# Half-row gathers on 128 partitions, a fourth k-step of expert 28 loaded ahead, and half of the last norm's row spread ahead of a product

## The chip, the core and the metric

One core of a Trainium2 chip runs the whole program. The metric is the device time of one execution in microseconds (us), as the median of several runs. Engines are named as in the profile: PE is TensorE, DVE VectorE, ACT ScalarE, POOL GpSimd, SP the queue engine that issues most DMAs; all DMAs of the core run on 16 DMA engines.

## The reference, cut to what matters

The program computes two blocks over 512 rows of 1024 numbers, all in fp32. The first block and the mixer of the second are not touched. Behind them stands a mixture of experts: 32 experts in 4 groups, 2 for each row, each with two matrices of 1024x512 (gate, up) and one of 512x1024 (down), then a last norm.

```python
h = rms_norm_2(x, norm_ffn_g) * (1.0 + sc_f) + sh_f
g = argmax(h @ w_router_group + b_group)                  # one of 4 groups
top_p, top_i = top_k(softmax(expert logits of group g), 2)
for each expert e, for the rows that chose it:
    hid = silu(rows @ w_gate[e]) * (rows @ w_up[e])       # 1024 -> 512
    y  += weight * (hid @ w_down[e])                      # 512 -> 1024
x = x + g_f * y
out = rms(x) * final_norm_g
```

Each expert's weights are 6 MB, 192 MB in all, and every one of them is read once from HBM.

## The kernel before, in words

**Tiles.** The rows of an expert are handled in a tile of at most 64 rows (MT = 64). Where more rows chose an expert, "extra" tiles follow on the same weights (`overflow`, `extras`). The router is a chain of small DVE steps and a few products on PE. At its end stands `slots` (lines 2678 to 2683): for each tile and each of its 64 places the number of the row that belongs there, made by a product of two one-hot tensors on PE (lines 2313 and 2314, 8 products that the profile shows as 16 instructions) and three DVE steps. Places that hold no row get a number past the end, which the gather leaves out. Rows fill a tile from place 0 upwards.

**Gather.** `dve_xn_tile` (line 785) scales the rows of the norm, and POOL stores them to a scratch in HBM (`xn_dram`, line 1960). For each tile POOL copies the tile's column of `slots` to `idx_col` and issues an indirect DMA (`gather`, lines 2891 to 2896): 64 indices, each a row of 4 KB, into 64 partitions of `tile.xg`.

**Turn.** `turn_rows` (line 2972) transposes the 64 gathered rows on PE, 8 transposes of 64x128 with a column stride of 8, into one PSUM bank; `rows_in` (line 3172) on DVE multiplies by the column of the norm's gain and adds the shift, and gives `tile.xT`.

**Products.** `gate_up` (line 2982) runs 8 k-steps of two products; `turn_hidden`, `down` (line 3006) follow. ACT makes the exponentials, DVE the rest (`clamped`, `hidden`, `rows_gated`), and POOL scatters the result with an indirect DMA of 128 half rows of 2 KB (`scatter`, line 2898). The PE stream for expert e is: turn the hidden tile of e-1, gate_up of e, turn the rows of e+1, down of e-1.

**Weights.** Three slots of 6 MB in SBUF (U = 3). SP issues loads in order (`sp_experts`, lines 2794 to 2880): the first three experts (in the order 1, 2, 0) as soon as the earlier phase frees the room, and then for each next expert the first half of gate and up (2 MB) when PE has done the first half of the product that used the slot before, the second half when the whole of it is done, and the down weights when that slot's down product is done. Each issue waits on a semaphore of PE, and the issues behind it on SP's queue wait with it. For expert 28 (AHEAD, the 29th) three of the eight k-steps (512 KB each) are loaded into a tensor of their own, `ahead`, much earlier (line 619), and only the fourth k-step of the first half is loaded in its turn (`load_behind_ahead`, line 2811). The last expert's second half comes as two quarters.

```python
def load_behind_ahead(u):
    eng.dma_start(wgu[u][:, 0, AHEAD_STEPS:4, :, :], A["w_gu"][AHEAD, :, 0, AHEAD_STEPS:4, :, :]
                  ).then_inc(w_gu[u][0], 16)
```

**Room.** `xg` of the three tiles are `yflat[0:64, 0:3072]`, that is yT, free once the mixer's output product is done; POOL clears them first (line 2887). `gain_row` and `ones_row`, for the last norm, lie on partition 64 of the same room.

**The end.** For the last expert (e = 31) PE runs turn_hidden and down of expert 30 ahead of gate_up of 31, and between them `spread_gain` (line 3085): two products that spread the 1024 gains of the last norm from one row to 128 partitions, which ACT copies to SBUF. When expert 30 is scattered, SP reads all results back (line 2872), DVE adds them (`add_rows`), PE sums with expert 31's rows straight from SBUF, and ACT and DVE make the last norm.

Of the kernel before, what the change touches and what calls it, by code (L numbers as in the profile page):

```python
# [75 lines left out]
def build_program(nc, A):  # L76
# [7 lines left out]
    with ctx:  # L84
# [696 lines left out]
        def dve_xn_tile(i, t):  # L781
            V.wait_ge(s_sq_rows, NORM0 + TT * (i - 1) + t + 1)
            if i == 2 and t >= 2:
                V.wait_ge(s_xnst, 16 * (t - 1))
            dve.done(V.tensor_scalar(xn_tiles[i - 1][t], X[:, t, :], rstd[:, t:t + 1], None, MUL))
            V.sem_inc(s_xn, 1)
# [1352 lines left out]
        def pe_block2(eng):  # L2139
# [173 lines left out]
            for n in range(2 * TT):  # L2313
                last = T.matmul(bank[0:MT, 0:NE + NOV], hot_pos[:, n, :], hot_tile[:, n, :], start=n == 0, stop=n == 2 * TT - 1)
# [273 lines left out]
        slots = sb("slots", [MT, NE + NOV + 2], u32)  # L2588
# [5 lines left out]
        xn_dram = nc.dram_tensor("xn_scratch", [SEQ, DM], fp32, kind="Internal").ap()  # L2594

# [6 lines left out]
        def dve_router(eng):  # L2602
# [76 lines left out]
            v = r_v[0:MT]  # L2679
            done(V.tensor_scalar(v, bank[0:MT, 0:NE + NOV], 0.0, 1024.0, ALU.is_equal, MUL))  # L2680
            empty(V, "dve", V.scalar_tensor_tensor(v, bank[0:MT, 0:NE + NOV], -1.0, v, ADD, ADD), ("slots",))
            done(V.tensor_copy(slots[:, 0:NE + NOV], v))
# [26 lines left out]

        def gate_up_weights(u, e, k):  # L2710

            if isinstance(e, int) and e == AHEAD and k < AHEAD_STEPS:
                return ahead[:, k, :, :]
            return wgu[u][:, k // 4, k % 4, :, :]
# [20 lines left out]
        tiles = [Tile(u, yflat[0:MT, 1024 * u:1024 * u + 1024], hflat[:, 512 * u:512 * u + 512],  # L2735
                      hflat[:, 1536 + 256 * u:1792 + 256 * u], yflat[:, 3072 + 256 * u:3328 + 256 * u],
                      hflat[:, 2304 + 512 * u:2816 + 512 * u]) for u in range(U)]
        extra = Tile("extra", side[0:MT, 0:1024], side[:, 1024:1536], side[:, 1536:1792], side[:, 1792:2048],
# [15 lines left out]
        idx_col = sb("idx_col", [MT, U + 1], u32)  # L2754
# [39 lines left out]
        def sp_experts(eng):  # L2794
# [16 lines left out]
            def load_behind_ahead(u):  # L2811
                eng.dma_start(wgu[u][:, 0, AHEAD_STEPS:4, :, :], A["w_gu"][AHEAD, :, 0, AHEAD_STEPS:4, :, :]
                              ).then_inc(w_gu[u][0], 16)

# [3 lines left out]
            def next_gate_up(u, e):  # L2818
# [6 lines left out]
                if isinstance(e, int) and e == AHEAD:  # L2825
                    load_behind_ahead(u)
                else:
# [27 lines left out]
            for u, e in enumerate(FIRST):  # L2855
# [3 lines left out]
                load_down(u, e)  # L2859
            eng.wait_ge(s_routed, 1)  # L2860
# [22 lines left out]
        def pool_experts(eng):  # L2883
            done = pool.done
            done(G.memset(ones_row, 1.0))
            eng.dma_start(gain_row, A["final_g"].rearrange("(o n) -> o n", o=1)).then_inc(s_gateB, 16)
            done(G.memset(yflat[0:MT, 0:3072], 0.0))
# [457 lines left out]
```

## Time and profile before

| what | us |
| --- | --- |
| median of 3 runs (1373.16 to 1378.31) | 1374.76 |
| the profiled execution | 1375.67 |
| its span, first to last instruction | 1374.0 |
| PE busy in the span | 1277.7 (93%) |
| DVE, ACT, POOL busy | 611.6, 351.0, 158.7 |
| mean granted clock of PE, of full speed | 0.976 |
| moved by DMA | 304.00 MB, of it 285.12 MB on SP's queue (q1) and 17.67 MB on POOL's (q0) |

The profiled execution lasts 1.7 us longer than its span, which counts from the first to the last instruction. In a window's row the busy times of the engines stand in us with the number of instructions in brackets; then the granted clock of PE as a share of full speed, the mean busy share of the 16 DMA engines, and GB/s. The share is a mean over the 16 engines: 0.5 can be half of them busy all the time, or all of them half the time. A share a little over 1 comes from the edges of a window. The name `arena` covers the three slots of weights, `yT` and `hT` the tiles' small tensors, `side` and `cactB` those of the extra tile. A product of fp32 shows as two matrix instructions, a transpose as one.

### The profile page before, as it was taken

The page shows a single profiled execution, that of the slowest core. Times are in us where ns is not written, and L with a number is a line of the kernel's source. Part 1 is how long each engine was busy: PE and PEld are TensorE (multiplying, and loading weights), DVE is VectorE, ACT ScalarE, POOL GpSimd, SP SyncE. Part 2 cuts the span into 40 slices and gives each one's busy share as a digit, 9 for nine tenths or more (in the row PEclk, how much of TensorE's full clock was granted, in tenths as well). Part 3 has the DMA queues.
Part 4 walks back from the last instruction along what each step waited for, and adds up shares of the span by engine and source line. Part 5 has one row for each costly group of instructions (what it writes and reads, how often), then busy time and mean ns, then how long its engine had stood idle before and what let it go on. Part 6 is the DMA issues. An engine that isn't in the chain of part 4 may idle for free.

```text
span 1374.0 us, 20748 instructions
## 1 busy us (share of the span) xinstructions
PE 1277.7 (93%) x7392; PEld 637.2 (46%) x7393; DVE 611.6 (45%) x1058; ACT 351.0 (26%) x759; POOL 158.7 (12%) x278
## 2 busy tenths in 40 slices
PE   5999999999999999999999999989989987897887
PEld 1446656678844444644455545433333333332322
DVE  1667787874223343268787525212212212122225
ACT  1323233321144442212478310111101101010112
POOL 4011111111010000000000002311121121121110
PEclk9999999999999999999999999999999999899999
DMA  9163624331191110042131565879999999999995
GB/s 373 66 261 78 231 73 169 140 108 43 36 293 47 46 31 0 0 159 77 52 142 50 199 264 208 306 313 394 407 416 420 401 401 421 404 408 405 403 389 214
DMA packets 40570, 304.00 MB, mean 221 GB/s; under 512 B 7980, under 2 KB 8132, under 8 KB 22944
## 3 DMA queue, kind: packets, MB, share of 16 engines
q1 hardware_dynamic: 31952, 285.12, 52.9%
q0 software_dynamic: 8528, 17.67, 4.2%
q8 instruction: 57, 0.93, 0.3%
q14 instruction: 33, 0.27, 0.1%
HBM read 299.49 MB, written 13.75 MB: 228 GB/s over the span
## 4 chain that ended last, share of the span: by engine, by line
PE 72%; DMA 12%; DVE 9%; ACT 3%; issue 2%; POOL 1%; DVEq 0%; ACTq 0%; SPq 0%; POOLq 0%
PE bank L886 19%; PE bank L2994 13%; DMA arena<-in_w_down 9%; PE bank L3012 8%; PE bank L817 8%; PE bank L932 3%; PE bank L994 2%; PE bank L2979 2%; DMA arena<-in_ada_w 2%; DVE side L1524 1%; PE bank L1008 1%; PE bank L1238 1%; PE bank L1182 1%; PE bank L1159 1%; DVE X L3271 1%
## 5 line engine op out<-in xcount | busy, mean ns | idle before, releaser
L886 PE MATMUL bank<-hT,arena 128*128 128x512 f32 x656 | 290.0, 597 | 0.0
L2994 PE MATMUL bank<-arena,hT 128*64 128x512 f32 x1012 | 229.1, 603 | 16.6 <-DMA arena<-in_w_gu 15.2
L886 PEld LDWEIGHTS bank<-hT,arena 128*128 128x128 f32 x656 | 122.8, 191 | 147.0 <-issue 143.5
L2994 PEld LDWEIGHTS bank<-arena,hT 128*64 128x64 f32 x1012 | 71.8, 138 | 153.7 <-issue 134.6
L3012 PE MATMUL bank<-arena,yT 128*64 128x512 f32 x512 | 125.5, 635 | 12.7 <-DMA arena<-in_w_down 10.9
L3182 DVE TENSOR_SCALAR hT<-hT 128x256 f32<-128x256 f32 x32 | 9.4, 294 | 246.7 <-ACT hT L3120 246.7
L817 PE MATMUL bank<-arena,yT 128*128 128x512 f32 x256 | 114.8, 603 | 2.4 <-DVE yT L1785 2.3
L3120 ACT ACTIVATE hT<-bank 128x256 f32<-128x256 f32 x32 | 12.3, 383 | 263.2 <-PE bank L2994 263.2
L817 PEld LDWEIGHTS bank<-arena,yT 128*128 128x128 f32 x256 | 48.2, 192 | 60.3 <-issue 56.5
L3012 PEld LDWEIGHTS bank<-arena,yT 128*64 128x64 f32 x512 | 36.5, 145 | 76.9 <-issue 62.4
L932 PEld LDWEIGHTS bank<-arena 64*64 64x64 f32 x1856 | 59.4, 135 | 23.5 <-issue 13.1
L932 PE MATMUL bank<-arena 64*64 64x64 f32 x1856 | 63.9, 220 | 3.0 <-ACT arena L1360 1.7
L706 POOL TENSOR_TENSOR arena<-arena 128x512 f32<-128x512 f32 x20 | 28.9, 1445 | 251.2 <-DVEq L1679 163.7
L1524 DVE SCALAR_TENSOR_TENSOR side<-arena,small,side 128x2048 f32<-128x2048 f32 x21 | 49.4, 2351 | 12.3 <-DMA arena<-in_ada_w 10.9
L3199 DVE TENSOR_TENSOR hT<-bank,masks 128x512 f32<-128x512 f32 x32 | 22.1, 692 | 70.5 <-PE bank L3012 70.3
L3128 ACT ACTIVATE yT<-bank 128x256 f32<-128x256 f32 x32 | 12.2, 383 | 135.9 <-PE bank L3003 135.9
L2362 DVE SCALAR_TENSOR_TENSOR arena<-arena,cols 128x512 f32<-128x512 f32 x60 | 45.1, 752 | 3.1
L2979 PEld LDWEIGHTS bank<-ident,yT 64*128 64x128 f32 x256 | 30.6, 201 | 32.6 <-issue 32.6
L2979 PE MATMUL bank<-ident,yT 64*128 64x64 f32 x256 | 34.8, 279 | 8.6 <-issue 7.8
L2900 POOL CAST place_col<-iotas 128x1 uint32 (+1 forms) x34 | 6.2, 183 | 279.4 <-DVE hT L3199 235.3
L1976 ACT ACTIVATE arena<-bank 128x512 f32<-128x512 f32 (+4 forms) x43 | 20.2, 470 | 69.5 <-PE bank L886 67.0
L1831 DVE TENSOR_TENSOR arena<-bank,arena 128x512 f32<-128x512 f32 x16 | 11.1, 691 | 59.3 <-PE bank L817 59.1
(498 smaller groups left out, 1697.3 us busy)
## 6 DMA issues: line engine op xcount, KB each, us to landing
arena<-in_w_gu SPq DMA_DIRECT2D x62, 2048.0 KB, 24.5
arena<-in_w_down SPq DMA_DIRECT2D x32, 2048.0 KB, 30.6
arena<-in_w_in SPq DMA_DIRECT2D x53, 512.0 KB, 3.6
arena<-in_ada_w SPq DMA_DIRECT2D x24, 1024.0 KB, 5.2
arena<-in_w_ada SPq DMA_DIRECT2D x8, 1024.0 KB, 9.4
arena<-in_w_out SPq DMA_DIRECT2D x8, 1024.0 KB, 9.3
arena<-in_w_ada SPq DMA_DIRECT2D x8, 512.0 KB, 7.4
arena<-expert_rows SPq DMA_DIRECT2D x4, 1024.0 KB, 8.4
```

The source lines that it names most:

```text
L706: done(G.tensor_tensor(Lfc[l % 2], LTc, level_up[:, l:l + 1, 0:HD].to_broadcast([P, 8, HD]), MUL))
L817: ins = T.matmul(bank[:, :], yT[:, k, CH(t)], w_outs[i][:, w_out_at(i, k), 512 * half:512 * half + 512], start=first and not m, stop=last ...
L886: last = T.matmul(bank[0:rows, :], w[:, k, 0:rows], hT[:, k, :], start=k == 0, stop=k == KD - 1)
L932: last = T.matmul(bank[r, BK(m)], stat[r, m, :], mov[r, m, :], start=True, stop=True)
L994: last = T.matmul(bank[:, CH(t)], hT[:, k, CH(t)], w[:, k, :], start=k == 0, stop=k == KD - 1)
L1524: dve.done(V.scalar_tensor_tensor(mod_sum, ada_slots[slot], c, mod_sum, MUL, ADD))
L1976: empty(S, "act", S.activation(dst, bank[:, :] if src is None else src(bank), kw.pop("func", ACT.Copy), **kw), name)
L2362: dve.done(V.scalar_tensor_tensor(cv[:, i, :], un[:, i, j:j + SEQ], col("cm_conv_w_2", i * CONV_K + j), cv[:, i, :], MUL, ADD))
L2979: last = T.transpose(banks[bank][:, MT * k:MT * k + MT], tile.xg[:, k::KD], ident[0:MT, 0:MT])
L2994: last = T.matmul(banks[1 + ub][MT * h:MT * h + MT, :], tile.xT[:, k, :], weights[:, :, 256 * h:256 * h + 256], start=k == 0, stop=k == KD ...
L3012: last = T.matmul(banks[5 + (u if db is None else db)][MT * q:MT * q + MT, :], tile.hidT[:, j, h, :], wdn[u][:, a, 512 * q:512 * q + 512], ...
L3199: V.tensor_tensor(tile.yo, banks[5 + u][:, :], gate_rows, MUL).then_inc(steps.rows, 1)
```

## The change

It has three parts.

1. **Gathers by half rows.** The scratch is read as 1024 half rows of 2 KB. `slots` now has 128 partitions: places 0 to 63 name first halves, 64 to 127 second halves (the product for it is made for both halves of the partitions, 32 instructions in place of 16, and the last DVE step adds the column `half_row`, -4 or -3, and 2 in place of a cast). `xg` is 128 partitions by 512 columns. So that the turn gives the order that the weights want, `dve_xn_tile` writes the scaled rows with their columns regrouped (read in order, written with a stride of 128 elements). `turn_rows` is 4 transposes of 128x128, and `rows_in` reads the bank through a reordered view. POOL clears 128x1536 in place of 64x3072.
2. **A fourth k-step of expert 28 ahead.** The narrower `xg` frees columns 1536 to 2559 of `yflat`. SP issues the 512 KB load of that k-step into it behind the loads of the first three experts and before its wait for the router; `load_behind_ahead` and its load are gone, the waits of that step stay. The count that `gate_up` waits for on that slot's first half is one load lower from there on.
3. **Half of the gain ahead of the down product.** The gain row is loaded as two DMAs of 2 KB, the second behind the router's second mark; `ones_row` moves to a row of `last_row` in `side`, which nothing reads any more at that time. In the last body PE spreads one half before `finish` (the down product of expert 30) and the other behind it. It waits for `first.xT` of expert 31 first, because bank 0 holds that expert's turned rows.

```diff
@@ -782,7 +782,11 @@
-            dve.done(V.tensor_scalar(xn_tiles[i - 1][t], X[:, t, :], rstd[:, t:t + 1], None, MUL))
+            if i == 2:
+                dve.done(V.tensor_scalar(xn_tiles[1][t].rearrange("p (k m) -> p m k", k=KD),
+                                         X[:, t, :].rearrange("p (m k) -> p m k", k=KD), rstd[:, t:t + 1], None, MUL))
+            else:
+                dve.done(V.tensor_scalar(xn_tiles[i - 1][t], X[:, t, :], rstd[:, t:t + 1], None, MUL))
@@ -2311,7 +2315,8 @@
-                last = T.matmul(bank[0:MT, 0:NE + NOV], hot_pos[:, n, :], hot_tile[:, n, :], start=n == 0, stop=n == 2 * TT - 1)
+                for q in range(2):
+                    last = T.matmul(bank[MT * q:MT * q + MT, 0:NE + NOV], hot_pos[:, n, :], hot_tile[:, n, :], start=n == 0, stop=n == 2 * TT - 1)
@@ -2585,13 +2590,14 @@
-        slots = sb("slots", [MT, NE + NOV + 2], u32)
+        slots = sb("slots", [P, NE + NOV + 2], u32)
...
+        xn_half = xn_dram.rearrange("t (h n) -> (t h) n", h=2)
@@ -2676,10 +2682,9 @@
-            v = r_v[0:MT]
-            done(V.tensor_scalar(v, bank[0:MT, 0:NE + NOV], 0.0, 1024.0, ALU.is_equal, MUL))
-            empty(V, "dve", V.scalar_tensor_tensor(v, bank[0:MT, 0:NE + NOV], -1.0, v, ADD, ADD), ("slots",))
-            done(V.tensor_copy(slots[:, 0:NE + NOV], v))
+            done(V.tensor_scalar(r_v, bank[:, 0:NE + NOV], 0.0, 4.0 * SEQ, ALU.is_equal, MUL))
+            empty(V, "dve", V.scalar_tensor_tensor(r_v, bank[:, 0:NE + NOV], 2.0, r_v, MUL, ADD), ("slots",))
+            done(V.tensor_scalar(slots[:, 0:NE + NOV], r_v, half_row, 2.0, ADD, ADD))
@@ -2707,10 +2712,14 @@
+        ahead_last = yflat[:, 512 * U:512 * U + 1024].rearrange("p (a n) -> p a n", a=2)
+
...
+            if isinstance(e, int) and e == AHEAD and k == AHEAD_STEPS:
+                return ahead_last
@@ -2732,10 +2741,10 @@
-        tiles = [Tile(u, yflat[0:MT, 1024 * u:1024 * u + 1024], hflat[:, 512 * u:512 * u + 512],
+        tiles = [Tile(u, yflat[:, 512 * u:512 * u + 512], hflat[:, 512 * u:512 * u + 512],
...
-        extra = Tile("extra", side[0:MT, 0:1024], side[:, 1024:1536], side[:, 1536:1792], side[:, 1792:2048],
+        extra = Tile("extra", side[:, 0:512], side[:, 1024:1536], side[:, 1536:1792], side[:, 1792:2048],
@@ -2751,7 +2760,7 @@
-        idx_col = sb("idx_col", [MT, U + 1], u32)
+        idx_col = sb("idx_col", [P, U + 1], u32)
@@ -2808,10 +2817,6 @@
-            def load_behind_ahead(u):
-                eng.dma_start(wgu[u][:, 0, AHEAD_STEPS:4, :, :], A["w_gu"][AHEAD, :, 0, AHEAD_STEPS:4, :, :]
-                              ).then_inc(w_gu[u][0], 16)
-
@@ -2822,9 +2827,7 @@
-                if isinstance(e, int) and e == AHEAD:
-                    load_behind_ahead(u)
-                else:
+                if not (isinstance(e, int) and e == AHEAD):
@@ -2857,6 +2860,7 @@
+            eng.dma_start(ahead_last, A["w_gu"][AHEAD, :, 0, AHEAD_STEPS, :, :]).then_inc(s_x, 16)
@@ -2883,8 +2887,9 @@
-            eng.dma_start(gain_row, A["final_g"].rearrange("(o n) -> o n", o=1)).then_inc(s_gateB, 16)
-            done(G.memset(yflat[0:MT, 0:3072], 0.0))
+            final_g = A["final_g"].rearrange("(o n) -> o n", o=1)
+            eng.dma_start(gain_rows[0], final_g[:, 0:512]).then_inc(s_gateB, 16)
+            done(G.memset(yflat[:, 0:512 * U], 0.0))
@@ -2892,8 +2897,8 @@
-                eng.indirect_dma_start(tile.xg, None, xn_dram, bass.IndirectOffsetOnAxis(ap=idx_col[:, i:i + 1], axis=0),
-                                       bounds_check=SEQ - 1, oob_is_err=False).then_inc(tile.gathered, 16)
+                eng.indirect_dma_start(tile.xg, None, xn_half, bass.IndirectOffsetOnAxis(ap=idx_col[:, i:i + 1], axis=0),
+                                       bounds_check=2 * SEQ - 1, oob_is_err=False).then_inc(tile.gathered, 16)
@@ -2938,6 +2943,7 @@
+            eng.dma_start(gain_rows[1], final_g[:, 512:1024]).then_inc(s_gateB, 16)
@@ -2953,7 +2959,8 @@
-        gain_row, ones_row = yflat[64:65, 0:DM], yflat[64:65, DM:DM + P]
+        gain_rows = yflat[64:65, 512 * U + DM:512 * U + DM + 512], side[64:65, 512:1024]
+        ones_row = last_row[64:65, :]
@@ -2975,21 +2982,22 @@
-                for k in range(KD):
-                    last = T.transpose(banks[bank][:, MT * k:MT * k + MT], tile.xg[:, k::KD], ident[0:MT, 0:MT])
+                for j in range(KD // 2):
+                    last = T.transpose(banks[bank][:, CH(j)], tile.xg[:, CH(j)], ident[:, :])
...
-                    eng.wait_ge(s_x, 32)
+                    eng.wait_ge(s_x, 48)
...
-                        eng.wait_ge(w_gu[u][k // 4], (it + 1) * 16)
+                        loads = 1 if isinstance(e, int) and k == 0 and e >= AHEAD and e % U == AHEAD % U else 0
+                        eng.wait_ge(w_gu[u][k // 4], (it + 1 - loads) * 16)
@@ -3070,8 +3078,10 @@
+                    eng.wait_ge(first.xT, NE + 1)
+                    spread_gain(0)
                     finish(it0, u0, e - 1)
-                    spread_gain()
+                    spread_gain(1).then_inc(s_spread, 1)
@@ -3082,11 +3092,9 @@
-            def spread_gain():
-                eng.wait_ge(s_gateB, 16 + 48)
-                for half in range(2):
-                    spread = T.matmul(banks[4 * half][:, :], ones_row, gain_row[:, 512 * half:512 * half + 512], start=True, stop=True)
-                spread.then_inc(s_spread, 1)
+            def spread_gain(half):
+                eng.wait_ge(s_gateB, 80)
+                return T.matmul(banks[4 * half][:, :], ones_row, gain_rows[half], start=True, stop=True)
@@ -3164,7 +3172,7 @@
-            A2, B2 = (a.rearrange("p (k o) -> p k o", o=1).to_broadcast([P, KD, MT]) for a in (AB[2], modc[4]))
+            A2, B2 = (a.rearrange("p (q j o) -> p q j o", q=2, o=1).to_broadcast([P, 2, KD // 2, MT]) for a in (AB[2], modc[4]))
@@ -3172,9 +3180,10 @@
-                V.tensor_tensor(tile.xT, b3(banks[bank][:, :], MT), A2, MUL).then_inc(steps.xT_own, 1)
+                xT = tile.xT.rearrange("p (q j) m -> p q j m", q=2)
+                V.tensor_tensor(xT, banks[bank][:, :].rearrange("p (j q m) -> p q j m", q=2, m=MT), A2, MUL).then_inc(steps.xT_own, 1)
                 eng.wait_ge(steps.xT_own, n + 1)
-                V.tensor_tensor(tile.xT, tile.xT, B2, ADD).then_inc(steps.xT, 1)
+                V.tensor_tensor(xT, xT, B2, ADD).then_inc(steps.xT, 1)
@@ -3222,7 +3231,7 @@
-            eng.wait_ge(s_gateB, 16 + 48)
+            eng.wait_ge(s_gateB, 80)
```

## Rows read from the trace of the kernel before

**Rows 1.** Windows: busy of PE, PEld, DVE, ACT, POOL; PEclk, DMA share, GB/s

```profile
777.00:808.00 31.00, 31.00 (x86) 14.72 (x85) 9.93 (x16) 4.49 (x10) 1.07 (x2) 1.00 1.00 413
...
810.00:812.00 2.00, 2.00 (x13) 1.41 (x12) 0.72 (x2) 0.00 (x0) 0.00 (x0) 1.00 0.10 41
...
853.30:865.80 12.50, 11.05 (x61) 5.75 (x62) 4.79 (x10) 0.00 (x0) 7.82 (x14) 0.83 0.27 83
...
913.00:919.00 6.00, 4.67 (x22) 1.69 (x22) 1.38 (x2) 0.38 (x1) 1.20 (x2) 1.00 0.06 15
...
935.00:1110.00 175.00, 168.33 (x796) 62.11 (x792) 43.04 (x84) 22.02 (x55) 30.76 (x52) 0.97 1.01 409
1110.00:1300.00 190.00, 164.35 (x752) 59.60 (x752) 40.47 (x78) 20.79 (x52) 30.74 (x52) 0.96 1.01 407
...
1331.00:1335.00 4.00, 3.13 (x16) 0.97 (x14) 0.69 (x1) 0.38 (x1) 1.17 (x2) 1.00 0.85 360
1335.00:1339.00 4.00, 4.00 (x16) 1.29 (x14) 0.69 (x1) 0.10 (x1) 0.38 (x2) 1.00 0.68 281
1339.00:1343.00 4.00, 4.00 (x20) 1.29 (x18) 0.00 (x0) 0.99 (x2) 0.78 (x1) 1.00 0.50 209
1343.00:1347.00 4.00, 4.00 (x17) 1.36 (x14) 0.29 (x1) 0.71 (x2) 0.00 (x0) 1.00 0.20 86
```

**Rows 2.** Chain of waits, 1100 to 1374 us: start, us, what

```profile
1301.14 32.12 DMA arena<-in_w_down
...
1351.78 1.30 DVE X L3271
```

**Rows 3.** Windows, columns as in rows 1: a gather, then a scatter, alone

```profile
856.50:857.20 0.70, 0.32 (x1) 0.00 (x0) 0.67 (x2) 0.00 (x0) 0.31 (x1) 1.00 0.63 187
865.50:865.85 0.35, 0.35 (x6) 0.07 (x4) 0.00 (x0) 0.00 (x0) 0.00 (x0) 1.00 0.87 340
```

**Rows 4.** DMA issues of the page's kind: size, median us to landing

```profile
arena<-in_w_gu SPq DMA_DIRECT2D x1, 512.0 KB, 41.6
```

**Rows 5.** DMA queues, 850 to 860 and 940 to 1300 us: packets, MB, share

```profile
q0 software_dynamic: 240, 0.55, 18.4%
...
q0 software_dynamic: 4121, 5.77, 4.9%
```

**Rows 6.** Gathers (L2895), scatters (L2903): ns min/median/max; the first gather's landing

```profile
L2895 POOL DMA_INDIRECT yT<-xn_scratch,idx_col x32: 954/979/1032, 852.5 to 1305.2; - x32
...
L2903 POOL DMA_INDIRECT expert_rows<-hT,place_col x31: 977/1013/1028, 885.6 to 1338.8; - x31
...
DMA to landing us min/median/max: 4.2/4.2/4.2
```

**Rows 7.** Chain of waits: the transposes of 64x128 and of 128x128

```profile
884.01 1.02 PE bank L2979 x8
...
788.76 0.89 PE bank L811 x8
```

**Rows 8.** Timeline, 831 to 861 us: start, us, engine, line [idle before <-releaser]

```profile
832.91 0.75 DVE L785 TENSOR_SCALAR arena<-X,small 128x1024 f32<-128x1024 f32 x1 [2.29 <-ACTq L756]
833.87 0.31 DVE L2615 TENSOR_TENSOR side<-bank,small 128x144 f32<-128x144 f32 x1 [0.21 <-PE bank L2272]
...
849.25 1.13 PE L2314 MATMUL bank<-hT 128*64 128x48 f32 x16 [1.51 <-DVEq L2673]
...
850.88 0.18 DVE L2682 CAST slots<-side 64x48 uint32<-64x48 f32 x1
...
855.43 0.39 DVE L2691 TENSOR_SCALAR iotas<-hT,small 128x48 f32<-128x48 f32 x1
...
857.65 1.95 PE L2979 MATMUL bank<-ident,yT 64*128 64x64 f32 x16 [0.83 <-DVEq L3170]
```

**Rows 9.** Timeline of PE, 1331 to 1340 us

```profile
1333.30 3.65 PE L3012 MATMUL bank<-arena,yT 128*64 128x512 f32 x16 [0.87 <-DMA arena<-in_w_down]
1336.89 1.98 PE L3088 MATMUL bank<-yT 1*128 1x512 f32 x4
```

## The prediction

> **What bounds the kernel now.** I read first the stages in time [rows 1]: PE busy, granted clock, the busy share of the 16 DMA engines, GB/s. From 935 to 1300 us the share is 1.01 at 407 to 409 GB/s, while PE is busy 168 of 175 and then 164 of 190 us: the experts' weights stream without a gap, and the stream is the bound. It is thus worth knowing when it begins without a gap and what ends it. Before it the share is 0.27 from 853.3 to 865.8 and 0.06 from 913 to 919: there PE sets the pace, because a weight load waits until PE has let go of its slot. Second, the chain of waits at the end [rows 2]: the down weights of expert 30, issued at 1301.14, land 32.12 us later, and only then PE's down product starts (at 1333.30, 3.65 us [rows 9]); behind it come the scatter of its rows, the reading back of all results, DVE's sums and the output. So what sets the end is the landing of those weights.
>
> Third, how the stream dies away [rows 1]. The first stream (two experts, 777 to 810, no gather in it) stops sharply: share 1.00, then 0.10 in the next two microseconds after 810. The last one fades: 0.85, 0.68, 0.50, 0.20 in four stretches of 4 us from 1331 to 1347. A load is complete when its last engine is, so some engines are 16 us behind the first. Summed, 4 x (0.85+0.68+0.50+0.20) = 8.9 us of full work is left at 1331; shared evenly it would end at 1339.9, 7.1 us before 1347. What is uneven? The weight loads are not (first stream). The gathers are suspects: 64 indices, and the valid ones are the first rows of a tile. Alone on the engines, a gather holds a share of 0.63 for 0.7 us at 187 GB/s (0.131 MB), a scatter of 128 half rows 0.87 for 0.35 us at 340 GB/s (0.119 MB) [rows 3]. About the same bytes in twice the time, with over a third of the engines idle.
>
> **The change part by part.**
> (1) The fourth k-step of expert 28, 512 KB (0.524 MB), leaves the stream [rows 4] and is issued behind the first experts' weights. At 407 GB/s [rows 1] that takes 1.3 us out of the stream. It lands in the stretch whose share is 0.27, where 12.5 us hold 3.4 us of work: costs nothing there, except that the first gather shares engines with it (in 4). SP issues one DMA more there and one less at 1244; the wait on the first half's product stays, and the second half's load waits for a later event anyway. If the idle stretch were gone, the 1.3 us would only move.
>
> (2) The gathers. Same bytes, 128 descriptors of 2 KB. Lower bound of the gain: nothing (the halves fall on the same engines). Upper bound: all 7.1 us. I take 5.5: if the halves spread as the scatter's do, a tile of up to 32 rows is even, but a fuller tile again gives some engines twice; the first three gathers moved 0.55 MB, 45 rows of 4 KB each [rows 5], while 5.77 MB in 360 us of stream [rows 5], half of it gathers, is 29 rows for each of the 24 experts there. Issue on POOL is 0.98 us for 64 indices and 1.01 for the scatter's 128 [rows 6]: nothing. The rest of the stream can follow, since even the engines that end first show no gap before 1331. The Trainium skill (DMA: Bandwidth & Descriptors, The descriptor swizzle) gives engine = 8 x (partition >> 6) + ((partition >> 2) & 7) for a transfer over 128 partitions: rows 0 to 31 and 64 to 95, all 16 engines. The trace shows no single engine, but the scatter's 0.87 agrees. A rule speaks against: the same page (Where 436 GB/s comes from) says that for HBM to SBUF the memory side binds, at about 358 GB/s a core; by it an even spread gains nothing and the sum would be 1.6 us. The trace has 407 to 413 GB/s over whole stages [rows 1].
>
> (3) PE turns rows with 4 transposes of 128x128 instead of 8 of 64x128. The 8 take 1.02 us; 8 of 128x128 elsewhere take 0.89, so 4 take 0.45 [rows 7]: 0.57 less. Where the stream is full it buys nothing. Before the gap at 913 to 919 ends, four turns lie on PE's chain, the first at 857.65 [rows 8], one of them at 884.01 (a fifth, an extra tile's, lies beside ACT's work): 4 x 0.57 = 2.3 us sooner.
>
> (4) Against it, in the router's chain, which ends in the first turn at 857.65 (PE waits 0.83 for DVE) [rows 8]. The slots' product gets 16 more instructions: 16 took 1.13 us, so +1.13. Its last DVE step is a cast of 0.18 and becomes a scalar operation with a column, like one of 0.39: +0.2. The four scaled rows of the norm are written with a stride: 0.75 us now for 1024 elements [rows 8]; the nearest slow row is the 1.30 of a two-tensor step of that length [rows 2]. Three lie beside products; the last is followed by a wait for PE of 0.21 us [rows 8], so 0 to +0.34; I take 0.3. The Trainium skill (VectorE: DVE Perf Modes, What auto-detection actually checks) asks no unit stride of fp32's double mode; by it this term is nothing. First gather: 4.2 us to landing [rows 6], so 856.7, 0.9 before its use; the chain moves later too, the extra load shares the engines up to 1.3 us: +0.2 (0 to 1.3). Sum +1.83. With (3): -0.5 us for the stream's start.
>
> (5) Half the gain's spread goes ahead of expert 30's down product: one half is 1.98/2 = 1.0 us, and PE has 0.87 between the end of the turn (1332.44) and the weights' landing [rows 9]: +0.15. The other half saves 1.0 on expert 31, which is not on the chain: DVE first adds gathered results. POOL's clearing halves; its extra DMA issue delays gathers used over 15 us later: nothing. DVE's reordered read of PSUM: same elements, nothing.
>
> Sum: -1.3 - 5.5 - 0.5 + 0.15 = -7.1 us. The profiled execution took 1375.67 us (span 1374.0 and 1.7 around it), 0.9 over the median 1374.76. So 1368.6 for it, **1367.6** for the median. 0.5% is 6.9 us, to 1367.9: about what a measurement can tell from no change.
>
> **Rivals.**
> A, the forecast: even gathers pay. 1362 to 1370. For: the fade, the half shares. Chance 0.66.
> B, the spread stays uneven (the halves fall on the same engines, the fade comes from something else, or the memory side binds, the rule above): the change then does not do this part. -1.3 - 0.5 + 0.15 = -1.6: 1373.2, from 1371 to 1374. For: no view shows one engine; scatters go on being counted by tile too. Against: the sharp end of the first stream. Chance 0.28.
> C, slower: the start of the experts grows. Place: from the slots' product to the first turn. Price: the 1.63 of (4) without its gather, the whole extra load ahead of the first gather (1.3), and that gather's landing doubled with its descriptors (4.2 more, less the 0.9 in hand: 3.3): 6.2, against 1.3 + 2.3 of gains: +2.6, 1377.4. It needs B to hold too, and decides once the chain grows by over 3.5 us. Chance 0.06.
>
> **How the numbers follow.** Range 1361 to 1373: it takes in A with the full 7.1 and the kinder ends of (4), and most of B; A's own is 1362 to 1370. Under 1367.9 lies about three quarters of A: faster 0.50. Slower by over 6.9 us needs C with a further cost on top: 0.03. Same 0.47.
>
> **What would show it.** (1) no load of 512 KB late, one of 512 KB near 839, stream total smaller. (2) the share from 10 us before expert 30's down weights land should stay near 1.0 and then drop within some 6 us instead of 16. (3) groups of 4 transposes at 0.45 us. (4) slots' product near 2.3 us; the norm's rows 0.75 or 1.3; the first turn 1 to 2 us later, the load after the gap within 1 us of 918. (5) under 0.3 us between landing and product. I am wrong if the fade keeps its shape (B), or the gap before the stream widens by more than 3 us (C).

## The result and the profile after

The changed kernel takes 1355.95 us (median of 6 runs, 1351.13 to 1357.23) where the kernel before, run beside it, takes 1373.96 (median of 6 runs): a ratio of 0.9864, 95% interval 0.9844 to 0.9884. Five of those six lie from 1370.28 to 1378.31; the sixth, a slow run of 1479.11, is left out of the ratio. The gain is 18 us, where 7.1 were forecast, and the time is under the range of 1361 to 1373. The profiled execution took 1355.69 us, with a span of 1354.0.

Windows like those of [rows 1], of the kernel after (us, busy us of PE, PEld, DVE, ACT and POOL, then granted clock, DMA share, GB/s). The last four are the end of its stream, where [rows 1] has 1331 to 1347:

```profile
853.30:865.80 12.50, 9.60 (x64) 4.60 (x64) 5.70 (x14) 0.00 (x0) 7.83 (x12) 1.00 0.50 189
...
935.00:1110.00 175.00, 165.44 (x764) 55.76 (x760) 43.50 (x87) 23.47 (x59) 34.28 (x56) 0.99 1.01 422
1110.00:1290.00 180.00, 154.14 (x696) 51.58 (x698) 38.57 (x76) 19.74 (x50) 31.86 (x52) 0.98 1.01 426
...
1311.00:1315.00 4.00, 4.00 (x18) 1.27 (x16) 0.69 (x1) 0.38 (x1) 1.16 (x2) 1.00 0.95 394
1315.00:1319.00 4.00, 3.85 (x16) 1.15 (x14) 0.69 (x1) 1.09 (x2) 0.52 (x2) 1.00 0.75 317
1319.00:1323.00 4.00, 4.00 (x20) 1.38 (x16) 0.00 (x0) 0.00 (x0) 0.64 (x1) 1.00 0.53 220
1323.00:1327.00 4.00, 3.92 (x14) 1.16 (x12) 0.43 (x2) 1.22 (x3) 0.00 (x0) 1.00 0.32 130
```

Two things stand here. The share in the stream is 1.01 as before, but it moves 422 and 426 GB/s where it moved 409 and 407. And the stream fades as slowly as before: 0.95, 0.75, 0.53, 0.32 over 16 us. The forecast had it the other way round.

The DMA view of the stretch from 940 to 1300 us has the moved GB/s in 40 slices of 9 us, and under it packets and bytes; the queues follow with packets, MB and share (q1 is SP's, which carries the weights, q0 POOL's). First the kernel before, whose queues stand in [rows 5]:

```profile
GB/s 423 371 389 414 408 427 423 423 404 412 424 419 420 416 384 420 402 396 406 417 374 418 427 401 430 428 422 423 362 407 386 398 428 392 412 422 398 424 377 399
DMA packets 13921, 146.91 MB, mean 408 GB/s; under 512 B 3790, under 2 KB 3790, under 8 KB 5336
```

The kernel after:

```profile
GB/s 424 416 432 423 422 428 388 408 428 429 423 427 419 423 430 420 430 423 429 424 427 427 422 433 428 422 422 426 425 427 426 423 429 421 430 422 426 422 421 427
DMA packets 14383, 152.60 MB, mean 424 GB/s; under 512 B 3951, under 2 KB 3951, under 8 KB 5431
...
q1 hardware_dynamic: 10049, 146.44, 96.1%
q0 software_dynamic: 4320, 5.98, 4.5%
```

Before, slices of 423 to 430 stand beside slices of 362 to 389, and the engines are over 90% busy in each; after, nearly all stand at 416 to 433. Divided out: the weights' queue moved 140.99 MB in 95.9% of 360 us, 408 GB/s for its own packets' time, and now 146.44 MB in 96.1%, 423 GB/s. The gathers' and scatters' own packets went from 5.77 MB in 4.9% to 5.98 MB in 4.5%, which is only 0.4% of 360 us, 1.4 us. So most of the gain is in packets that the change doesn't touch.

The chain of waits at the end of the kernel after (start, us, what) answers to [rows 2]:

```profile
1270.83 37.06 DMA arena<-in_w_down
...
1311.96 1.05 PE bank L3097 x2
1313.01 3.61 PE bank L3020 x16
...
1318.66 7.90 DMA expert_rows<-hT,place_col
...
1327.03 7.71 DMA arena<-expert_rows
```

The end is bound as before: the landing of down weights, the last two down products, the scatter, the reading back. The two profiled executions compare by three stretches. SP's load after the gap leaves at 916.71 (918.04 before): 1.3 us. From it to PE's down product of expert 30 (at 1312.94, before 1333.30 [rows 9]) it is 396.2 us in place of 415.3: 19.0 us. From there to the end of the span 41.1 in place of 40.7. Together 20.0, the difference of the spans. That middle stretch, called **the streaming stretch** below, came out within 0.3 us in the two kernels that were profiled twice (the changed one and the one of e8), while whole times of one kernel differ by up to 10; so the verdicts below rest on it as much as on the medians. It is one execution each time.

The stretch does not always hold the same bytes. In the kernel before it moved 168.30 MB, in the kernel after 167.21: 405 and 422 GB/s over the whole of it.

### The profile page after: what moved, and what is told of

It reads as the page before. It is cut to its first block, busy times and chain, and to the rows that moved or that the text cites. A ratio compares the mean times of both kernels' runs of the same rounds, so it can differ in the third digit from the quotient of the medians.

```text
span 1354.0 us, 20494 instructions
## 1 busy us (share of the span) xinstructions
PE 1254.0 (93%) x7264; PEld 616.7 (46%) x7265; DVE 611.8 (45%) x1058; ACT 351.0 (26%) x759; POOL 161.3 (12%) x279
## 4 chain that ended last, share of the span: by engine, by line
PE 68%; DMA 15%; DVE 9%; ACT 3%; issue 3%; POOL 1%; DVEq 0%; SPq 0%; ACTq 0%; POOLq 0%
PE bank L890 19%; DMA arena<-in_w_down 12%; PE bank L3002 12%; PE bank L821 8%; PE bank L3020 7%; PE bank L936 3%; PE bank L998 2%; DMA arena<-in_ada_w 2%; DVE side L1528 2%; PE bank L1242 1%; PE bank L1186 1%; PE bank L1012 1%; PE bank L1163 1%; PE bank L2986 1%; PE bank L925 1%
## 5 line engine op out<-in xcount | busy, mean ns | idle before, releaser
L3020 PE MATMUL bank<-arena,yT 128*64 128x512 f32 x512 | 118.1, 603 | 14.6 <-DMA arena<-in_w_down 12.0
L2900 POOL DMA_INDIRECT yT<-xn_scratch,idx_col x32 | 33.7, 1054 | 30.6 <-POOL idx_col L2897 23.0
L1835 DVE TENSOR_TENSOR arena<-bank,arena 128x512 f32<-128x512 f32 x16 | 11.1, 692 | 57.4 <-PE bank L821 57.3
L1663 DVE TENSOR_TENSOR arena<-bank,arena 128x512 f32<-128x512 f32 x32 | 22.1, 692 | 30.9 <-PE bank L936 30.0
```

What stands on the lines that cost most here:

```text
L1663: empty(V, "dve", V.tensor_tensor(dst, b3(bank[:, :], HD), dst, ADD), (n, p, l))
L2900: eng.indirect_dma_start(tile.xg, None, xn_half, bass.IndirectOffsetOnAxis(ap=idx_col[:, i:i + 1], axis=0), bounds_check=2 * SEQ - 1, oob_ ...
L3020: last = T.matmul(banks[5 + (u if db is None else db)][MT * q:MT * q + MT, :], tile.hidT[:, j, h, :], wdn[u][:, a, 512 * q:512 * q + 512], ...
```

## Experiments

The theories are: **S**, the gathers onto 64 partitions slow the weights' own packets; **U**, some engines get more than others; **D**, the 4 KB rows slow them; **H** (from e5 on), the rows' data must itself go over both halves of the partitions. S was formed from the slices above.

**e1, the gathers alone.** The changed kernel with parts 2 and 3 undone:

```diff
+                    load_behind_ahead(u)
...
-            eng.dma_start(ahead_last, A["w_gu"][AHEAD, :, 0, AHEAD_STEPS, :, :]).then_inc(s_x, 16)
...
-                    spread_gain(0)
                     finish(it0, u0, e - 1)
+                    spread_gain(0)
                     spread_gain(1).then_inc(s_spread, 1)
```

> The changed kernel with its second and third parts undone: expert 28's fourth k-step is again loaded late, as 512 KB of the stream, and both halves of the last norm's row are spread behind expert 30's down product. What stays is the gathers onto 128 partitions and all that hangs on them. Theory S (the 64-partition gathers slowed the weights' own packets around them): the stream's rate stays that of the changed kernel, 422 to 426 GB/s against 407 to 409, so nearly the whole gain of 18 us stays: 1357 to 1359 us, ratio to before 0.988. Theory P (the gain is the sum of many small parts, the ahead load among them): 1362 or more. The late load of 0.52 MB at 424 GB/s costs 1.2 us either way.

1354.51 us, ratio 0.9866 (0.985 to 0.9881); 423 and 425 GB/s in the two long windows; streaming stretch 397.2 us, with 167.27 MB. The whole gain is there with part 1 alone. Parts 2 and 3 add nothing to it that shows in the time.

**e3, twice the descriptors.** The kernel before, the scratch stored as two arrays of half rows, and each gather as two of 64 indices:

```diff
-                eng.indirect_dma_start(tile.xg, None, xn_dram, bass.IndirectOffsetOnAxis(ap=idx_col[:, i:i + 1], axis=0),
+                for h in range(2):
+                    eng.indirect_dma_start(tile.xg[:, 512 * h:512 * h + 512], None, xn_dram[h], bass.IndirectOffsetOnAxis(ap=idx_col[:, i:i + 1], axis=0),
...
```

> The kernel before, with each gather split into two indirect DMAs of 64 indices, each with rows of 2 KB (the left and the right half of the rows, from two scratch arrays), onto the same 64 partitions. Twice the descriptors, each as large as those of the changed kernel, but on 64 partitions. Theory S (the gathers' 64 partitions slow the weights' packets): stays at the rate of before, 407 to 410 GB/s, time 1374 to 1378 (POOL issues one DMA more per tile, about 1 us, off the chain but for the first). Theory D (the 4 KB rows slow them): rate 420 or more, 1358 to 1364.

1376.04 us, ratio 1.0018 (1.0006 to 1.0029), 406 GB/s in both windows, streaming stretch 415.1 us. D falls: rows of 2 KB on 64 partitions cost what rows of 4 KB cost, and twice as many descriptors by themselves help nothing.

**e4, other places, still 64 partitions.** The kernel before, the comparison that makes `hot_pos` reads its numbers in another order:

```diff
-            done(V.tensor_tensor(hot_pos, to_rows(iota, KT, MT), per_row(r_pos, MT), ALU.is_equal))
+            done(V.tensor_tensor(hot_pos.rearrange("p n (g j) -> p n g j", j=4),
+                                 iota.rearrange("p (o j g) -> p o g j", o=1, j=4).to_broadcast([P, KT, 16, 4]),
+                                 r_pos.rearrange("p (n a b) -> p n a b", a=1, b=1).to_broadcast([P, KT, 16, 4]), ALU.is_equal))
```

> The kernel before with the places of e2 (rank r at place 4*(r mod 16) + r div 16), gathers still of 64 rows of 4 KB onto 64 partitions. Theory S: rate stays at 407 to 410 GB/s, time 1372 to 1376. Theory U (the uneven load of the engines by the first rows of a tile is what costs, in the stream as in the fade): the rate rises toward 420 and the time falls by 6 to 15 us, 1359 to 1368.

1372.59 us, ratio 0.9994 (0.9981 to 1.0007), 409 and 408 GB/s, streaming stretch 412.2 us. U falls as the cause of the slow stream: with the valid rows spread over the 64 partitions the rate is what it was. The stretch is 3.1 us shorter, 1.9 of it because it holds 0.79 MB less (167.51 in place of 168.30). Nor do spread places alone end the fade. Windows of 2 us near the end of e4's stream:

```profile
1332.00:1334.00 2.00, 1.87 (x10) 0.73 (x12) 0.00 (x0) 0.00 (x0) 0.98 (x1) 1.00 0.97 414
...
1336.00:1338.00 2.00, 2.00 (x6) 0.57 (x7) 0.53 (x1) 0.27 (x1) 0.55 (x2) 1.00 0.68 284
...
1340.00:1342.00 2.00, 2.00 (x12) 0.60 (x10) 0.00 (x0) 0.00 (x0) 0.00 (x0) 1.00 0.49 207
...
1344.00:1346.00 2.00, 2.00 (x7) 0.68 (x4) 0.29 (x1) 0.85 (x3) 0.00 (x0) 1.00 0.27 115
```

**e5, 128 partitions in form only.** The kernel before; `xg` and `idx_col` of tiles 1 and 2 have 128 partitions, the upper 64 indices name no row:

```diff
-        tiles = [Tile(u, yflat[0:MT, 1024 * u:1024 * u + 1024], hflat[:, 512 * u:512 * u + 512],
+        tiles = [Tile(u, yflat[0:P if u else MT, 1024 * u:1024 * u + 1024], hflat[:, 512 * u:512 * u + 512],
...
+            done(G.memset(slots[MT:P, 0:NE + NOV], 4 * SEQ))
...
```

> The kernel before, with the gathers of tiles 1 and 2 addressed to 128 partitions: the lower 64 indices and rows of 4 KB as before, the upper 64 indices all out of range, so that they move nothing. Tile 0's gathers and the extra tile's stay on 64 partitions. Theory S (it is the form of the transfer, 64 partitions, that slows the weights' packets): two thirds of the gathers are cured, the rate rises by two thirds of the way from 408 to 424, to about 418 GB/s, time about 1364, and slices of 4 us with a gather of tile 0 stay slow while those of tiles 1 and 2 are not. Theory H (what matters is that the data itself goes over both halves of the partitions): the valid rows still land on partitions 0 to 63, the rate stays at 407 to 410, time 1373 to 1377. Theory D (rows of 4 KB) expects the same as H, but fell with the last runs.

The DMA view of 940 to 1290 us, then the windows of the long stretches:

```profile
GB/s 432 424 418 427 412 416 419 394 420 421 395 430 428 425 423 382 425 427 426 403 421 430 419 419 420 436 429 423 422 422 432 380 420 428 419 410 427 424 426 424
DMA packets 14837, 146.81 MB, mean 419 GB/s; under 512 B 4740, under 2 KB 4740, under 8 KB 6249
```

```profile
935.00:1110.00 175.00, 166.59 (x802) 61.62 (x798) 43.03 (x83) 22.04 (x55) 31.67 (x52) 0.98 1.01 415
1110.00:1290.00 180.00, 157.26 (x730) 57.37 (x730) 38.17 (x73) 19.60 (x49) 31.59 (x52) 0.96 1.01 422
```

The rate is 419, as S has it (418). The data lands on the same 64 partitions in rows of the same size; what differs is the form of the transfer, with 64 empty packets in each (9872 packets on POOL's queue in place of 8528, 64 more for each of 21 gathers, and the same bytes). Inside this one execution I took the 4 us from 3 to 7 us after each issue of a gather: the 16 gathers of tiles 1 and 2 have a mean of 428 GB/s in them (412 to 440), the 8 of tile 0, still on 64 partitions, 394 (360 to 431). That is not a trait of tile 0: in the kernel before the windows of the same 16 gathers have a mean of 392, those of the same 8 have 383, all 24 together 389 (355 to 426). In the kernel after 25 have 426 (411 to 447), in e4 24 have 397. The extra tile's two gathers, also on 64 partitions, are left out of these means: they moved 0.00 MB, and behind them the kernel before shows 422 and 418, so it takes a gather with rows in it to slow the stream. This is the most direct showing of S, and H falls with it.

The time is 1368.31 us, ratio 0.9958 (0.9941 to 0.9975), 5.6 us under the kernel before beside it: less of a gain than the 10 us expected. The streaming stretch is 407.7 us, 7.6 less than before. Part of what is missing shows in the end of the stream, which is down to a share of 0.83 from 1322 on, 6 us before PE's down product of expert 30 (1328.22); in the kernel before that comes 2 us before it (0.85 from 1331 on, 1333.30). The windows there:

```profile
1322.00:1326.00 4.00, 3.46 (x21) 1.61 (x22) 2.43 (x5) 1.07 (x3) 0.00 (x0) 1.00 0.83 354
1326.00:1330.00 4.00, 3.17 (x18) 0.98 (x16) 0.69 (x1) 0.38 (x1) 1.17 (x2) 1.00 0.57 240
1330.00:1334.00 4.00, 4.00 (x16) 1.28 (x14) 0.69 (x1) 0.18 (x1) 0.46 (x2) 1.00 0.43 178
1334.00:1338.00 4.00, 4.00 (x20) 1.29 (x18) 0.00 (x0) 0.91 (x2) 0.70 (x1) 1.00 0.32 133
1338.00:1342.00 4.00, 4.00 (x17) 1.31 (x14) 0.29 (x1) 0.68 (x2) 0.00 (x0) 1.00 0.19 79
```

A long thin tail: some engines carried more than others, which is what the data of two thirds of the gathers on half of the partitions would do if the engine follows from the partition.

**e6 and e7, the dose.** Gathers of tiles 1 and 2 issued twice, the second copy where nothing reads it, first on 64 partitions in the kernel before, then on 128 in the kernel of e1:

```diff
-                eng.indirect_dma_start(tile.xg, None, xn_dram, bass.IndirectOffsetOnAxis(ap=idx_col[:, i:i + 1], axis=0),
+                for to in (tile.xg,) + tile.again:
+                    eng.indirect_dma_start(to, None, xn_dram, bass.IndirectOffsetOnAxis(ap=idx_col[:, i:i + 1], axis=0),
...
```

> The kernel before, with every gather of tiles 1 and 2 issued twice, the second copy onto partitions 64 to 127 beside the first, where nothing reads it. About 1.9 MB more in the stream (two thirds of half of the 5.58 MB of the software queue), which at 408 GB/s is 5 us. Theory S: each gather onto 64 partitions costs the weights' packets time beside its own bytes, 15 us for all of them, so two thirds more of them cost 10 us on top: rate about 400 GB/s, time about 1389. If only the bytes counted: 1379, rate 408.

> The control of the run before: the kernel of e1 (half-row gathers on 128 partitions alone), with every gather of tiles 1 and 2 issued twice, the second copy onto 128 partitions of spare room, where nothing reads it. Theory S: only the bytes count here, 1.9 MB at 424 GB/s, 4.5 us: 1359, rate 424 GB/s. If any gather slows the weights by its descriptors or its turn at the memory, whatever its form, the rate falls here too, to 416 or less, and the time is 1366 or more.

e6: 1394.64 us, ratio 1.0162 (1.0134 to 1.019), 396 GB/s. e7: 1363.27 us, ratio 0.9932 (0.9905 to 0.9959), 422 and 424 GB/s. In the streaming stretch the doubled gathers moved 2.1 MB more on POOL's queue (8.65 in place of 6.57 in e6, 8.66 in place of 6.57 in e7), near the 1.9 of the expectation. With what the stretch holds in all, e7 moved 169.96 MB in 403.6 us and e1 167.27 in 397.2: 421 GB/s both times, so on 128 partitions a gather costs its bytes. (The other 3 us of e7 lie before the stretch, where the first turn of tile 1 waits 2.21 us for the doubled gather; that is why its time is over the 1359 expected.) On 64 partitions the stretch is 17.8 us over that of the kernel before (433.1 and 415.3) and its rate falls from 405 to 394 GB/s. The 2.1 MB at 408 GB/s are 5.1 of those, all that it moved more (170.62 in place of 168.30 MB) 5.7: some 12 us beyond the bytes for two thirds of the gathers, where S had 10. So the copies, onto partitions 64 to 127, must do it too.

**e2, spread places on 128 partitions.** The edit of e4 on the changed kernel.

> The changed kernel with an expert's rows given other places in its tile: rank r goes to place 4*(r mod 16) + r div 16, so that the valid rows of a gather, and of the scatter of the results, lie spread over the 64 places instead of in the first of them. Same bytes, same instructions but for the order in which one DVE comparison reads its row of numbers. Theory U (the 14 us fade at the end comes from gathers and scatters that load some engines more than others): the fade shrinks to some 8 us, and the end comes 3 to 6 us sooner: 1350 to 1353. Theory S (evenness plays no part; what matters is the 64-partition form): within 2 us of the changed kernel, 1354 to 1358, the stream's rate 422 to 426 GB/s as before.

1349.19 us (1346.11 to 1354.57), ratio 0.9819 (0.9802 to 0.9837), just under the range of U and well under that of S. Streaming stretch 392.6 us, 3.7 less than the changed kernel's. **e8** is the same on e1:

> The places of e2 on the kernel of e1: half-row gathers on 128 partitions and spread places, with the load of expert 28's fourth k-step late again and both halves of the norm's row spread behind the down product. Against e2 (1349.2) it tells what these two parts are worth when the stream ends sharply. If the early load is worth its bytes (0.52 MB at 424 GB/s, 1.2 us) and the early half costs its 1.05 us on PE between landing and product: the same as e2 within 1 us. If the two cost more than they give, as e1 against the changed kernel hints (1354.5 against 1355.9): 1347 to 1348.

1347.69 us (1345.63 to 1354.92), ratio 0.9826 (0.9799 to 0.9853), streaming stretch 392.8 against e1's 397.2. The windows at the end of its stream, the last of which holds the first of the reading back:

```profile
1308.00:1312.00 4.00, 4.00 (x14) 1.15 (x12) 0.69 (x1) 0.78 (x2) 0.84 (x2) 1.00 0.99 414
1312.00:1316.00 4.00, 4.00 (x22) 1.29 (x18) 0.00 (x0) 0.30 (x1) 0.32 (x1) 1.00 1.02 433
1316.00:1320.00 4.00, 4.00 (x16) 1.16 (x12) 0.38 (x2) 1.22 (x3) 0.00 (x0) 1.00 0.52 214
```

The fade of 16 us is gone: full to 1316, over some 3 us later. So U was right about the fade, though not about the stream. It takes both edits: the half-row form alone leaves the fade (the kernel after), and so do spread places alone (e4). The first would follow if an engine serves certain partitions: the first places are the first partitions of both halves. No view shows a single engine, so that stays an argument.

**e9 to e12, the two small parts.** Four kernels beside each other: the changed kernel again, and with spread places: the early load alone, the early half alone, neither.

> The changed kernel itself, run beside the next three on the same chip so that they can be compared: 1355 to 1357 us, ratio to before about 0.987.

> Half-row gathers on 128 partitions and spread places (e8), plus the early load of expert 28's fourth k-step; both halves of the norm's row spread behind the down product. By the bytes: the load leaves 0.52 MB out of the stream, 1.2 us less than e8's 1347.7, so 1346.5. If it only delays the first gathers by what it takes out later, as the pair of the changed kernel and e1 hints: the same as e8 or up to 2 us more, 1348 to 1350.

> Half-row gathers on 128 partitions and spread places (e8), plus the early half of the norm's row; the k-step is loaded late. In the traces so far the path from the end of the turn to expert 30's down product is 1.31 us without the half (e8) and 1.42 with it (the changed kernel), so it costs 0.1 us: 1347.8. If it costs its whole 1.05 us on PE: 1348.7.

> e8 again, beside e9 to e11: 1347 to 1349, 7 to 9 us under the changed kernel. If spread places are worth less than that, as e2's 1349.2 allows: 5 to 7.

| kernel | places | early load, early half | median us (lowest to highest) | ratio | streaming stretch |
| --- | --- | --- | --- | --- | --- |
| after | first | yes, yes | 1355.95 (1351.13 to 1357.23) | 0.9864 | 396.2 |
| e9 | first | yes, yes | 1353.93 (1352.75 to 1354.94) | 0.9865 | 396.3 |
| e1 | first | no, no | 1354.51 (1353.81 to 1356.47) | 0.9866 | 397.2 |
| e2 | spread | yes, yes | 1349.19 (1346.11 to 1354.57) | 0.9819 | 392.6 |
| e10 | spread | yes, no | 1349.73 (1348.22 to 1352.51) | 0.9839 | 390.6 |
| e11 | spread | no, yes | 1347.76 (1347.75 to 1352.56) | 0.9834 | 391.8 |
| e8 | spread | no, no | 1347.69 (1345.63 to 1354.92) | 0.9826 | 392.8 |
| e12 | spread | no, no | 1353.57 (1347.94 to 1355.6) | 0.9866 | 392.5 |

e12 misses its expectation (1347 to 1349, here 1353.57), though its kernel is e8's: its profiled execution took 1347.94, the three timed ones 1352.7 to 1355.6. These medians therefore tell no 2 us apart. Over all runs, the 15 of the three kernels with first places have a mean of 1354.5 us and the 25 of the five with spread places 1350.0, with standard errors of 0.5 and 0.6: spread places are worth some 4.5 us, and the stretch agrees (3.7 for e2 against the changed kernel, 4.4 for e8 against e1). Any of them beats both the kernel before and the changed one; which of them is best is not settled. The early load shortens the stretch by 2.0 us (e10 against e8 and e12) or lengthens it by 0.8 (e2 against e11), and the ten runs that have it with spread places have the same mean as the fifteen that don't (1350.0). With first places the stretch is 0.9 to 1.0 us shorter where both small parts are in (the changed kernel and e9 against e1). What the early load is worth is less than these runs tell from nothing.

## Why the prediction was wrong, step by step

**What bounds the kernel: right**, and it held after the change. The streaming stretch carries 19.0 of the 20.0 us.

**Step (2), the gathers: the failed step.** I put their price at the fade alone, "upper bound: all 7.1 us", and took 5.5 for engines evened out. Neither holds: the fade is as long as before, and part 1 takes 18.1 us out of the streaming stretch (415.3 to 397.2 in e1). 415.3 us at 424 in place of 408 GB/s are 15.7 of those; the other 2.4 are bytes, because e1's stretch holds 1.03 MB less (167.27 in place of 168.30), which at 421 GB/s are 2.4 us. A sharp end, once it was had (e2, e8), shortened the stretch by 3.7 to 4.4 us, where I had taken 5.5. That the kernel came out faster as forecast, by the very part that I named, is luck as far as the mechanism goes. The reasoning error was to read a share of 1.01 as a stream at its ceiling. A share counts the time that packets are under way, not what they carry (1.01 at 408 and at 424 GB/s), so packets slowed by others look like a full engine. Two rows pointed there. [Rows 3]: the gather alone moved 187 GB/s at a share of 0.63, so 297 per full share, and the scatter 340 at 0.87, 391. I read there only that a third of the engines idled. [Rows 1]: 413 GB/s in the stream without gathers, 407 to 409 with them. The difference understates the loss (the stream with gathers now moves 424, so 413 was no ceiling), but slices of 362 and 430 GB/s side by side, on which the prediction did not draw, show it.

**Why the 64-partition form slows others** is not shown: no view has a single engine. Shown is that it isn't the size of rows or the number of descriptors (e3), the places (e4), or which partitions receive data (e5), and that it grows with the number of such gathers (e6). The Trainium skill (SBUF — State Buffer, Door 1: The DMA port swizzle) gives 16 ports into SBUF, of which partitions 0 to 63 reach eight; by that rule alone e5, whose data goes to those same partitions, should be as slow as before, and it is not. Together with the Trainium skill's map of engines that the prediction named (DMA: Bandwidth & Descriptors, The descriptor swizzle), in which each engine of a 128-partition transfer has a port of its own, the runs would fit: in a 64-partition transfer all engines share eight ports and meet the weights of others there. That is an argument, not a finding. The Trainium skill's rule on the memory side, which I held against the change (DMA: Bandwidth & Descriptors, Where 436 GB/s comes from: about 358 GB/s a core), binds nothing here: the stream runs at 424.

**Step (1), the early load: -1.3 forecast, no gain found.** Its bytes leave the stream (0.9 to 1.0 us of the stretch, above), but the first gather can pay: in the kernel after the first turn waits 1.27 us for the gather, in e9 1.42, while in e1, without the load, it waits 0.81 for DVE. From the router's last product to the first gate_up that is 29.7 and 29.9 us against 29.2; I had put 0.2 for it. With spread places (e2, e10) that wait is not there, and where the load's 1.2 us then go stays open; a difference in the clock, below, is as large.

**Steps (3) and (4), turns and router chain: the sign right, the sum too small, terms off.** Rows of the timeline of the kernel after:

```profile
834.91 1.32 DVE L786 TENSOR_SCALAR arena<-X,small 128x1024 f32<-128x1024 f32 x1 [2.30 <-ACTq L756]
...
851.77 1.14 PE L2319 MATMUL bank<-hT 128*64 128x48 f32 x32 [1.51 <-DVEq L2679]
...
853.44 0.25 DVE L2687 TENSOR_SCALAR slots<-side,small 128x48 uint32<-128x48 f32 x1
...
854.70 1.87 PE L2326 MATMUL bank<-hT 128*64 128x48 f32 x32 [0.74 <-DVEq L2692]
...
859.76 0.63 PE L2986 MATMUL bank<-ident,yT 128*128 128x128 f32 x4 [1.27 <-DMA yT<-xn_scratch,idx_col]
...
861.90 1.51 PE L3002 MATMUL bank<-arena,hT 128*64 128x512 f32 x6 [0.50 <-DVE hT L3186]
```

The slots' product has 32 instructions and takes 1.14 us, as 16 did in 1.13: my +1.13 is nothing. The strided norm rows take 1.32 in place of 0.75 us, and PE's wait behind the last of them grows from 0.45 to 0.97: +0.5, over my 0.3 and its upper end of 0.34; the Trainium skill's rule (VectorE: DVE Perf Modes, What auto-detection actually checks), which asks no unit stride of fp32's double mode and would have made this term nothing, does not hold for this row. Cast to scalar: 0.18 to 0.25, not +0.2. The products for the places take 1.87 in place of 2.83, at a granted clock of 1.00 from 848 to 856 where before it was 0.79. That varies from run to run: with the router of before e6 has 1.87 too, and with that of after e2 has 2.65. From the router's last product (832.17) to the first gate_up it is 29.7 us, 30.05 before (830.17 to 860.22): -0.3 where I had +1.8. To the load after the gap it is 84.5 us in place of 87.9: 3.3 sooner, where (3) and (4) gave 0.5. The first gate_up product stands in the two chains, after and before, as

```profile
861.90 7.09 PE bank L3002 x32
```

```profile
860.22 8.78 PE bank L2994 x32
```

so 1.7 of the 3.3 are a product at a higher granted clock (1.00 from 856 to 864, before 0.82), and that varies too among kernels with the change (e2 and e9 have 0.81 and 0.79 there). The next turns take 0.59 and 0.44 us on the chain in place of 1.02 each, near the 0.45 forecast. The whole start came only 1.3 us sooner because the run reached the router 2.0 us later, which varies between runs (828.7 to 834.5 over the traces). That the measured 1.3 is not far from my 0.5 is luck: two things that I had not foreseen, the product's clock and the later router, nearly cancel.

**Step (5), the early half: +0.15 forecast, 0.1 found.** From the turn of the hidden tile to the down product of expert 30:

```profile
1311.52 0.44 PE L3011 MATMUL bank<-ident,hT 128*128 128x128 f32 x2
1311.89 1.12 PE L3097 MATMUL bank<-yT,side 1*128 1x512 f32 x2
1312.94 3.65 PE L3020 MATMUL bank<-arena,yT 128*64 128x512 f32 x16
```

1.42 us from the start of the turn to the product; without the half (e8) 1.31, from 1304.31 to this row:

```profile
1305.62 3.65 PE L3022 MATMUL bank<-arena,yT 128*64 128x512 f32 x16 [0.87 <-DMA arena<-in_w_down]
```

**Rivals.** B had the fade right (it keeps its shape) and its time wrong, for the reason of step (2); C's place did not grow (8.4 us from the slots' product to the first turn, now 8.0). The case that happened, a faster stream at the same share, was not among my cases, and so the range, whose low end was set by the 7.1 us of the fade, could not hold it.

## To carry to other kernels

A DMA share of 1.0 is not a rate: divide bytes by share, slice by slice, and compare slices with and without the small transfers before calling a stream full. Where weights stream on all engines beside indirect gathers, try the gathers in the 128-partition form, even where half of the indices name nothing, and with it spread the valid rows over the partitions, so that the stream also ends sharply. Here the first was worth 18 us of 1374 and the second some 4.5 more, both for transfers that carry 4% of the bytes. With half of the indices empty, on two thirds of the gathers, it was 5.6 (e5); spread places without the 128-partition form gave nothing that the times show (e4).

## What the runs showed that I had not expected

PE's granted clock falls from 904 to 912 us in most of the traces, and a down product there takes 6.21 us in place of 3.65 (the kernel before has one of 6.29 at 906.92). The kernel after and e8, window of 904 to 912 and PE's timeline:

```profile
904.00:912.00 8.00, 7.01 (x20) 2.29 (x20) 0.37 (x1) 0.38 (x1) 0.52 (x1) 0.57 0.73 309
...
905.68 6.21 PE L3020 MATMUL bank<-arena,side 128*64 128x512 f32 x16 [0.57 <-ACT side L3136]
```

```profile
904.00:912.00 8.00, 7.04 (x32) 2.73 (x34) 0.69 (x1) 0.64 (x2) 1.20 (x2) 1.00 0.61 253
...
904.40 3.65 PE L3022 MATMUL bank<-arena,side 128*64 128x512 f32 x16 [0.56 <-ACT side L3138]
```

In e8, e11 and e12 the fall comes after 920, where the stream has PE waiting anyway, and their load after the gap leaves 81.6 to 82.3 us after the router's last product began, against 84.1 to 85.0 in the other kernels of 128 partitions (e7, with its doubled gathers, aside). Among the kernels of 64 partitions e3 is the one without the fall, and has 85.8 against 87.9 to 88.7. So 2 to 3 us hang on where the clock falls, twice what the early load was meant to give. Before the fall PE had waited 2.33 us for DVE at an extra tile, but it did so in e8 as well; what decides where the fall comes was not tried.

Two matrix products into the two halves of the partitions, issued in turn, took the time of one at the same granted clock of 1.00: 32 instructions in 1.14 us, 16 in 1.13. And a DVE step of 128x1024 fp32 took 1.32 us with a strided output and 0.75 with a plain one.
